# First block's borders by token tiles and column halves, roots with a prepared bias, the MLP's last turn by tiles

## The chip, the cores and the metric

One core of a Trainium2 chip runs the whole program. The metric is the device time of one execution in microseconds (us). TensorE (PE in the rows) does matmuls and transposes, VectorE (DVE) and ScalarE (ACT) the elementwise work, GpSimd (POOL) a little of it, and SyncE (SP) issues all the DMAs, which land in SBUF.

## The reference

Three blocks follow one another on x, 256 tokens of 1024 channels in float32; this case touches only the first, a transformer block of two layers with three kinds of attention. Of each layer, cut to what matters here:

```python
for l in range(DEPTH):                       # DEPTH = 2
    h = _rms_norm(x, norm_mix_pre[l])
    proj = jnp.einsum('bsd,de->bse', h, w_in[l])
    ...                                      # three attentions on parts of proj, gated and mixed
    mixed = jnp.einsum('bsd,de->bse', jnp.sum(gates * br, axis=2), w_out[l])
    x = x + _rms_norm(mixed, norm_mix_post[l])
    h = _rms_norm(x, norm_mlp_pre[l])
    u = jnp.square(jax.nn.relu(jnp.einsum('bsd,df->bsf', h, w_up[l])))
    x = x + _rms_norm(jnp.einsum('bsf,fd->bsd', u, w_down[l]), norm_mlp_post[l])
```

`_rms_norm(x, w)` is `x * rsqrt(mean(x*x) + 1e-6) * w` over the 1024 channels of a token. The second ("even") block begins with a projection of the x that the first leaves.

## The kernel before

Tokens stand in two tiles of 128 partitions (t = 0, 1). Every float32 product is made from three fp32r matmuls (`product`, L379): high times high, low times high and high times low. Weights come in pieces of about 1 MB, each into one of four slots. `load_piece` (L313) issues a piece's DMA on SyncE once the piece that was four before it in the slot is "used"; `high_of_next` (L333) has ScalarE copy it, rounded, into the high part (L344, two halves of 1024 columns), and `low_of_next` (L346) has VectorE subtract that for the low part (L357). Both functions are called at fixed places of each engine's program, two pieces ahead of their use; each engine runs its instructions strictly in program order and waits on counting semaphores. PSUM has 8 banks, which `claim` gives out in turn.

"Border" means here the stretch from the last product of one stage to the first product of the next. There are four of this kind: in each layer from `w_out` ("wo") to the MLP (two), from the first layer's MLP to the second layer's projections, and from the second layer's MLP to the even block. At the first three the same steps follow one another for all 256 tokens at once: ScalarE squares the four banks (two tiles by two column halves, `weigh_scalar`, L1318) with their sums kept, VectorE multiplies them by the norm's weight (`weigh_vector`, L982), a root is made from the sums (`rstd_vector` and `rstd_scalar`: L486, L493, L488), VectorE adds the normed result to x (L994, one instruction of 1024 columns for each tile), ScalarE squares tile 0 of the new x (L1305) and VectorE tile 1 (L965), again a root, VectorE scales both tiles (L970), TensorE transposes them in groups of four 128x128 squares (`turn_tensor`, L459), ScalarE copies the high parts out of PSUM (L468) and VectorE makes the low parts (L478). At the fourth border x is transposed without a norm.

The rows of norm weights are broadcast over the partitions by DMAs of 512 KB. `f.pre` and `f.post` serve both norm pairs, so their MLP rows are issued only when the mix norms are through ("weighed"), and the next layer's pre row when the layer is done ("layer_done").

The MLP runs eight turns. In each TensorE makes two `up` pairs (48 matmuls of 256 columns each) and then multiplies two `down` pieces, j = 0 and 1, with the hidden values, each piece for both tiles and both column halves into four banks held through all turns (`mlp_tensor`, L903). ScalarE and VectorE make the hidden values in between (L1474, L1261, L1479, L1263).

Of the kernel before, what the change touches and what calls it, by code (L numbers as in the profile page):

```python
# [14 lines left out]
P = 128  # L15
S = 256
TT = S // P
D = 1024
# [186 lines left out]
class Kernel:  # L205
# [120 lines left out]

    def load_beyond(self, name):
# [197 lines left out]

FILL_ORDER = [0, 1, 2, 3, 4, 5, 6, (0, 0), (0, 1), 7, 8, 9, (1, 0), (1, 1), 10, 11]
# [15 lines left out]
class FirstPlaces:  # L542
    def __init__(self, k, x):
# [13 lines left out]
        self.stats = take(64)  # L557
# [7 lines left out]
        self.qnT, self.knT = take(4, S), take(4, S)  # L565
        self.heads_out = split(self.pre, TT, WB)
# [29 lines left out]
def first_pieces(k):  # L596
# [8 lines left out]
    for l in range(DEPTH):  # L605
        wi, wo, wu, wd = w_in[:, l], w_out[:, l], w_up[:, l], w_down[:, l]
        for n in range(6):
# [5 lines left out]
            if n == 2:  # L613
# [22 lines left out]
def first_sync(k, f):  # L636
# [13 lines left out]
    for l in range(DEPTH):  # L650
        if l:
            SP.wait_ge(("layer_done", l - 1))
            nc.sync.dma_start(f.pre, row("norm_mix_pre", l)).then_inc(*k.pre_loaded("pre_loaded", l))
# [30 lines left out]
def first_tensor(k, f):  # L684
    nc, T, table = k.nc, k.T, k.table
    for l in range(DEPTH):
        projections_tensor(k, f, l)
        attention_tensor(k, f, l)
        for half in range(2):
            k.token_major(("wo", l, half), k.halves_of(("wo", l, half)), f.hT, WB, lambda t, kk: [("mixed", l, kk // 2 * 2)])  # L690
        k.turn_tensor(("normed", "mlp", l), split(f.flat_junk, TT, D), KT, [[("normed_by", "mlp", l, t)] for t in range(TT)])
        mlp_tensor(k, f, l)

# [18 lines left out]
def projections_tensor(k, f, l):  # L712
    nc, T = k.nc, k.T
    T.wait_ge(("tables_loaded",))
    k.turn_tensor(("normed", "mix", l), split(f.flat_junk, TT, D), KT, [[("normed_by", "mix", l, t)] for t in range(TT)])
    h_ready = k.turned("normed", "mix", l)
    for n in range(6):
        if n in (2, 5):
# [6 lines left out]
        if n == 2:  # L725
# [177 lines left out]
def mlp_tensor(k, f, l):  # L903
    nc, T = k.nc, k.T
    acc = [k.claim("mlp", l, t, half, bank=2 * t + half) for t in range(TT) for half in range(2)]
    for i in range(TURNS):
        for j in range(2):
            k.pair(("up", l, i, j), ("up", l, i, j), f.hT, k.turned("normed", "mlp", l), bank=4 + j)
        for j in range(2):
            p, w = k.weights(("down", l, i, j), 2, D)  # L910
            T.wait_ge(("hidden", l, i, j))
            first, last = i + j == 0, (i, j) == (TURNS - 1, 1)
            for t in range(TT):
                for half in range(2):
                    for kk in range(2):
                        ins = k.product(acc[2 * t + half], [part[:, kk, t * P:(t + 1) * P] for part in f.hidden[j]],
                                        [part[:, kk, half * WB:(half + 1) * WB] for part in w], first and kk == 0, last and kk == 1)
                    if last:
                        ins.then_inc(*T("mlp", l, t, half))
# [25 lines left out]
def first_vector(k, f):  # L945
    nc, V = k.nc, k.V
    nc.vector.memset(f.rel, 1.0).then_inc(*V("rel_ones"))
    for l in range(DEPTH):
        projections_vector(k, f, l)
        attention_vector(k, f, l)  # L950
        for half in range(2):
            k.low_of_next()
            k.low_of_next()
            weigh_vector(k, f, ("mix", l), half, [("wo", l, half, t) for t in range(TT)], ("post_loaded", l))
        add_normed_vector(k, f, ("mix", l))
        normed_vector(k, f, ("mlp", l), ("mlp_rows_loaded", l))
# [3 lines left out]
def normed_vector(k, f, tag, weight_loaded, *ready, pieces=0):  # L960
# [8 lines left out]
    for t in range(TT):  # L969
        nc.vector.scalar_tensor_tensor(normed[:, t, :], x[:, t, :], f.stats[:, 2 + t:3 + t], f.pre, ALU.mult, ALU.mult  # L970
                                       ).then_inc(*V("normed_by", *tag, t))
# [5 lines left out]
def weigh_vector(k, f, tag, half, uses, post_loaded):  # L977
    nc, V = k.nc, k.V
    for t in range(TT):
        at = t * D + half * WB  # L980
        V.wait_ge(("squared", *tag, half, t), post_loaded)
        nc.vector.tensor_tensor(f.flat_junk[:, at:at + WB], k.bank(*uses[t]), f.post[:, half * WB:(half + 1) * WB], ALU.mult  # L982
                                ).then_inc(*V("weighed", *tag, half, t))
        V.same("free", *uses[t])


def add_normed_vector(k, f, tag):
    nc, V, stats, x = k.nc, k.V, f.stats, f.x
    sums = split(stats[:, 0:4], 2, 2)
    nc.vector.tensor_tensor(stats[:, 4:6], sums[:, :, 0], sums[:, :, 1], ALU.add).then_inc(*V())  # L990
    k.rstd_vector(("add", *tag), stats[:, 6:8], stats[:, 4:6], D, EPS_RMS, V)
    V.wait_ge(V)
    for t in range(TT):
        nc.vector.scalar_tensor_tensor(x[:, t, :], f.flat_junk[:, t * D:(t + 1) * D], stats[:, 6 + t:7 + t], x[:, t, :],  # L994
                                       ALU.mult, ALU.add).then_inc(*V("added_to_x", *tag, t))


def projections_vector(k, f, l):
    nc, V, stats = k.nc, k.V, f.stats
    if l == 0:  # L1000
        normed_vector(k, f, ("mix", l), ("pre_loaded", l), ("x_loaded",), pieces=1)
        for _ in range(AHEAD - 1):
            k.low_of_next()
    else:
        normed_vector(k, f, ("mix", l), ("pre_loaded", l))
    for n in range(6):
# [14 lines left out]
        if n == 2:  # L1021
# [232 lines left out]
def mlp_vector(k, f, l):  # L1254
# [11 lines left out]
    for half in range(2):  # L1266
        weigh_vector(k, f, ("mlp", l), half, [("mlp", l, t, half) for t in range(TT)], ("mlp_rows_loaded", l))
    add_normed_vector(k, f, ("mlp", l))
    V.same("layer_done", l)
# [5 lines left out]
def first_scalar(k, f):  # L1275
    nc, A = k.nc, k.A
    for l in range(DEPTH):
        projections_scalar(k, f, l)
        attention_scalar(k, f, l)
        for half in range(2):  # L1280
            k.high_of_next()
            k.high_of_next()
            weigh_scalar(k, f, ("mix", l), half, [("wo", l, half, t) for t in range(TT)])
        k.rstd_scalar(("add", "mix", l), f.stats[:, 6:8])
# [2417 lines left out]
```

## Time and profile before

| | |
|---|---|
| three runs | 1819.9, 1815.75, 1820.47 us; median 1819.9 |
| profiled execution | 1820.19 us, its span 1818.9 us |
| PE busy | 1634.9 us, 90% of the span |
| DVE busy | 1139.2 us, 63% |
| ACT busy | 767.5 us, 42% |
| DMA | 219.94 MB, mean 121 GB/s |
| mean granted TensorE clock | 0.921 |

The span is from the first to the last instruction of the profiled execution; its own time adds 1.3 us around it. Busy shares are means over three blocks with different limits, so what a border costs is read from the timelines of that stretch. Of the chain that ended last, PE holds 72%, DVE 17%, ACT 7% and DMA 3%. In a row of a timeline the brackets give the idle time of the engine before it and what ended it.

### The profile page before, as it was taken

The numbers are of one execution on the slowest core, as the hardware profiler recorded it, in microseconds if no ns is written. First come the engines' busy times: TensorE is split into PE (matmuls) and PEld (weight loads), VectorE is DVE, ScalarE is ACT, GpSimd is POOL, SyncE is SP. The second block draws the span as 40 slices with busy tenths as digits, with TensorE's granted clock in tenths as the row PEclk, the third lists the DMA queues.
The fourth block names the chain that finished last, engine by engine and source line by source line (L and its number), as shares of the span: only waits on it lengthen the run. The fifth ranks groups of instructions, "written<-read, shape, count | busy, mean of one in ns | idle before, by whom it ended". The sixth has DMA issues, their size and how long they took to land.

```text
span 1818.9 us, 24216 instructions
## 1 busy us (share of the span) xinstructions
PE 1634.9 (90%) x10180; PEld 1435.5 (79%) x10180; DVE 1139.2 (63%) x1898; ACT 767.5 (42%) x1260; POOL 53.1 (3%) x50
## 2 busy tenths in 40 slices
PE   7988997999989899979999998987799888999887
PEld 6978886999889888869998987766789767785455
DVE  5577556555546665465556668454977757777765
ACT  4545434444434454344444463422312234645334
POOL 0000011000000000100000001000000000000000
PEclk9999999999989899889999999966877799899998
DMA  8543334555545433245556532000002065331041
GB/s 268 164 140 124 109 105 162 178 189 186 186 136 170 132 122 114 95 139 185 185 186 192 183 110 77 1 1 1 1 1 94 0 209 156 114 129 45 23 156 70
DMA packets 151181, 219.94 MB, mean 121 GB/s; under 512 B 6230, under 2 KB 110686, under 8 KB 150432
## 3 DMA queue, kind: packets, MB, share of 16 engines
q1 hardware_dynamic: 151072, 218.39, 37.6%
q8 instruction: 80, 1.31, 0.3%
q14 instruction: 29, 0.24, 0.0%
HBM read 217.31 MB, written 1.06 MB: 120 GB/s over the span
## 4 chain that ended last, share of the span: by engine, by line
PE 72%; DVE 17%; ACT 7%; DMA 3%; issue 1%; SPq 0%; DVEq 0%
PE bank L381 17%; PE bank L383 16%; PE bank L382 16%; DVE weights_low L357 4%; PE bank L1901 4%; PE bank L846 2%; PE bank L1992 2%; PE bank L3227 2%; ACT weights_high L344 2%; PE bank L2187 2%; DVE place L2381 1%; PE bank L459 1%; PE bank L1958 1%; DMA place<-ple_w_dram 1%; PE bank L3188 1%
## 5 line engine op out<-in xcount | busy, mean ns | idle before, releaser
L357 DVE TENSOR_TENSOR weights_low<-place,weights_high 128x1024 fp32r<-128x1024 f32 (+2 forms) x387 | 450.1, 1206 | 189.4 <-ACT weights_high L344 188.9
L344 ACT ACTIVATE weights_high<-place 128x1024 fp32r<-128x1024 f32 (+2 forms) x387 | 378.7, 1031 | 140.7 <-DMA place<-w_down_dram 42.9
L381 PE MATMUL bank<-hT_high,weights_high 128*128 128x256 f32 x1152 | 336.7, 292 | 6.6 <-DVE hT_low L478 5.0
L383 PE MATMUL bank<-hT_high,weights_low 128*128 128x256 f32 x1152 | 329.2, 286 | 0.0
L382 PE MATMUL bank<-hT_low,weights_high 128*128 128x256 f32 x1152 | 328.7, 285 | 0.0
L381 PEld LDWEIGHTS bank<-hT_high,weights_high 128*128 128x128 f32 x1152 | 222.1, 193 | 12.7 <-DVE hT_low L478 5.8
L382 PEld LDWEIGHTS bank<-hT_low,weights_high 128*128 128x128 f32 x1152 | 221.9, 193 | 0.6
L383 PEld LDWEIGHTS bank<-hT_high,weights_low 128*128 128x128 f32 x1152 | 221.3, 192 | 0.0
L1901 PE MATMUL bank<-place,place 128*128 128x128 f32 x624 | 90.8, 312 | 26.2 <-DVE place L2348 10.4
L1901 PEld LDWEIGHTS bank<-place,place 128*128 128x128 f32 x624 | 87.0, 224 | 33.4 <-issue 22.6
L381 PE MATMUL bank<-weights_high,branchT_high 128*128 128x512 f32 x256 | 101.0, 395 | 0.0
L383 PE MATMUL bank<-weights_high,branchT_low 128*128 128x512 f32 x256 | 101.0, 394 | 0.0
L382 PE MATMUL bank<-weights_low,branchT_high 128*128 128x512 f32 x256 | 101.0, 394 | 0.0
L1424 ACT ACTIVATE place<-place,place 128x256 f32<-128x256 f32 x40 | 20.4, 510 | 144.8 <-DVE place L1155 144.8
L459 PE MATMUL bank<-place,place 128*128 128x128 f32 x144 | 28.1, 367 | 54.5 <-DVE place L970 39.8
L459 PEld LDWEIGHTS bank<-place,place 128*128 128x128 f32 x144 | 24.7, 196 | 58.9 <-DVE place L970 30.9
L1261 DVE TENSOR_TENSOR place<-place 128x512 f32<-128x512 f32 x32 | 22.2, 692 | 74.7 <-ACT place L1474 74.7
L381 PE MATMUL bank<-hT_even_high,weights_high 128*128 128x256 f32 x208 | 61.1, 294 | 3.8 <-DVE weights_low L357 2.5
L381 PE MATMUL bank<-weights_high,hT_high 128*128 128x512 f32 (+1 forms) x160 | 62.1, 388 | 0.8 <-DVE place L1243 0.8
L383 PE MATMUL bank<-weights_high,hT_low 128*128 128x512 f32 (+1 forms) x160 | 61.8, 386 | 0.0
L381 PE MATMUL bank<-branchT_high,weights_high 128*128 128x256 f32 x192 | 57.7, 301 | 4.5 <-ACT place L1401 2.3
L382 PE MATMUL bank<-weights_low,hT_high 128*128 128x512 f32 (+1 forms) x160 | 61.7, 386 | 0.0
(416 smaller groups left out, 3377.1 us busy)
## 6 DMA issues: line engine op xcount, KB each, us to landing
place<-w_in_dram SPq DMA_DIRECT2D x48, 1024.0 KB, 5.3
place<-w_up_dram SPq DMA_DIRECT2D x32, 1024.0 KB, 5.5
place<-w_down_dram SPq DMA_DIRECT2D x32, 1024.0 KB, 5.0
place<-even_w_in_dram SPq DMA_DIRECT2D x17, 1024.0 KB, 5.3
place<-w_out_dram SPq DMA_DIRECT2D x16, 1024.0 KB, 5.1
place<-odd_w_in_dram SPq DMA_DIRECT2D x16, 1024.0 KB, 5.3
place<-w_branch_dram SPq DMA_DIRECT2D x12, 1024.0 KB, 5.0
place<-ple_gate_dram SPq DMA_DIRECT2D x8, 1024.0 KB, 5.9
```

The lines of the kernel that those rows point to most:

```text
L344: nc.scalar.activation(high[:, lo:hi], self.raw[p % SLOTS][:, lo:hi], ACT.Copy).then_inc(*A("high", p, j))
L357: nc.vector.tensor_tensor(low[:, lo:hi], self.raw[p % SLOTS][:, lo:hi], high[:, lo:hi].bitcast(FP32), ALU.subtract).then_inc(*V())
L381: nc.tensor.matmul(out, left[0], right[0], start=first, stop=False)
L382: nc.tensor.matmul(out, left[0], right[1], start=False, stop=False)
L383: return nc.tensor.matmul(out, left[1], right[0], start=False, stop=last)
L459: ins = nc.tensor.transpose(out, tile, self.table("ident"))
L846: ins = nc.tensor.matmul(b[:, at_:at_ + keys], qT[:, q0:q0 + P], kT[:, 0:keys], start=j == 0, stop=j == len(pairs) - 1)
L1261: nc.vector.tensor_tensor(f.u[j], f.u[j], f.u[j], ALU.mult).then_inc(*V("squared_u", l, i, j))
L1901: ins = nc.tensor.matmul(b[:, h * P:(h + 1) * P], left(h), right(h), start=True, stop=True)
L1992: ins = nc.tensor.matmul(b[out, i * width:(i + 1) * width], mats[rows, u, out], right[rows, i, :], start=True, stop=True)
L2187: ins = nc.tensor.matmul(b[:, h * 64:(h + 1) * 64], M[:, h, which, :], right[:, h * 64:(h + 1) * 64], start=not step and j == 0, stop=j == ...
L3227: ins = nc.tensor.matmul(b, left[:, tile, t, :], o.mag[n][hf][:, 0 if real else 1, t, :], start=t == 0, stop=t == TT - 1)
```

## The change

The three borders inside the first block and the one behind it are worked tile by tile and in column halves of 512.

- The second column half of `w_out` is multiplied by `by_tiles_tensor`: tile 0 over both pieces, then tile 1 (before: the first piece for both tiles, then the second). The MLP's last turn likewise: tile 0 with both `down` pieces, then tile 1.
- Weigh, add, square and scale are issued for each tile, in halves. Of each root the mean with epsilon of one column half is prepared on VectorE (`first_mean`), and ScalarE's Sqrt takes it as bias and the other half's sum as input with a scale.
- All squares of the new x are on ScalarE. A Sqrt of one column is put on ScalarE ahead of `w_out`'s first cuts.
- The MLP's norm rows get places of their own (`mlp_pre`, `mlp_post`, over `qnT` and `knT`), and all norm rows are issued earlier in SyncE's queue.
- The cut of the second `up` piece is moved from ahead of the border to behind it.
- The second layer's projections begin with n = 2 (values, token-major) by tiles, and tile 1's transposes are put between its two pieces.

The diff, cut to its core; `weigh_scalar` and the scalar engine's loops are split like the vector engine's.

```diff
+PROJECTIONS = ((0, 1, 2, 3, 4, 5), (2, 0, 1, 3, 4, 5))
...
+        self.mlp_pre, self.mlp_post = (a.rearrange("p a b -> p (a b)") for a in (self.qnT, self.knT))
...
-        k.load_beyond(("wo", l, 1, 1))
-        SP.wait_ge(("weighed", "mix", l, 1, 1), ("headsT", l, 2, 3))
-        nc.sync.dma_start(f.pre, row("norm_mlp_pre", l)).then_inc(*rows())
-        nc.sync.dma_start(f.post, row("norm_mlp_post", l)).then_inc(*rows("mlp_rows_loaded", l))
-        k.load_beyond(("down", l, TURNS - 1, 1))
+        k.load_up_to(("wo", l, 1, 1))
+        SP.wait_ge(("headsT", l, 2, 3))
+        nc.sync.dma_start(f.mlp_pre, row("norm_mlp_pre", l)).then_inc(*rows("mlp_rows_loaded", l))
+        k.load_beyond(("down", l, 0, 1))
+        nc.sync.dma_start(f.mlp_post, row("norm_mlp_post", l)).then_inc(*k.pre_loaded("mlp_post_loaded", l))
+        if l + 1 < DEPTH:
+            nc.sync.dma_start(f.pre, row("norm_mix_pre", l + 1)).then_inc(*k.pre_loaded("pre_loaded", l + 1))
+        SP.wait_ge(("weighed", "mix", l, 1, 1))
+        if l + 1 == DEPTH:
+            k.load_beyond(("down", l, TURNS - 1, 1))
...
+def by_tiles_tensor(k, f, name, ready, between=None):
+
+    T = k.T
+    for t in range(TT):
+        b = k.claim(*name, t)
+        for j, (part, m) in enumerate(k.halves_of(name)):
+            if between and (t, j) == (0, 1):
+                between()
+            p, w = k.weights(part, m, WB)
+            for kk in range(j * m, (j + 1) * m):
+                T.wait_ge(*ready(t, kk))
+                ins = k.product(b, [x[:, kk, t * P:(t + 1) * P] for x in f.hT], [x[:, kk - j * m, :] for x in w], kk == 0, kk == KT - 1)
...
-        for j in range(2):
+        end = i == TURNS - 1
+        for t, j in [(t, j) for t in range(TT) for j in range(2)] if end else [(None, j) for j in range(2)]:
...
+        k.low_of_next()
+        weigh(1, 0)
+        add_normed_vector(k, f, ("mix", l), 0)
+        normed_vector(k, f, ("mlp", l), f.mlp_pre, 0, ("mlp_rows_loaded", l))
+        weigh(1, 1)
+        add_normed_vector(k, f, ("mix", l), 1)
+        k.turn_vector(("normed", "mlp", l), f.hT, KT, 0, [0])
+        normed_vector(k, f, ("mlp", l), f.mlp_pre, 1, ("mlp_rows_loaded", l))
+        k.turn_vector(("normed", "mlp", l), f.hT, KT, 0, [4])
+        k.turn_vector(("normed", "mlp", l), f.hT, KT, 1)
+        k.low_of_next()
         mlp_vector(k, f, l)
...
+def normed_vector(k, f, tag, weight, t, weight_loaded):
+
+    nc, V, stats = k.nc, k.V, f.stats
+    V.wait_ge(("square", *tag, t, 0))
+    nc.vector.tensor_scalar(stats[:, 52 + t:53 + t], stats[:, 48 + 2 * t:49 + 2 * t], 1.0 / D, EPS_RMS, ALU.mult, ALU.add
+                            ).then_inc(*V("first_mean", "norm", *tag, t))
+    V.wait_ge(("deviation", "norm", *tag, t))
+    nc.vector.reciprocal(stats[:, 54 + t:55 + t], stats[:, 54 + t:55 + t]).then_inc(*V())
+    V.wait_ge(V, weight_loaded)
+    for half in range(2):
+        at, cut = t * D + half * WB, slice(half * WB, (half + 1) * WB)
+        nc.vector.scalar_tensor_tensor(f.flat_junk[:, at:at + WB], f.x[:, t, cut], stats[:, 54 + t:55 + t], weight[:, cut],
+                                       ALU.mult, ALU.mult).then_inc(*V("normed_by", *tag, t, half))
...
+        nc.scalar.activation(f.stats[:, 64:65], k.table("ones")[:, 0:1], ACT.Sqrt).then_inc(*A())
...
+    nc.scalar.activation(stats[:, 6 + t:7 + t], stats[:, 2 * t + 1:2 * t + 2], ACT.Sqrt, scale=1.0 / D, bias=stats[:, 4 + t:5 + t]
+                         ).then_inc(*A("deviation", "add", *tag, t))
```

On VectorE, from the last cuts of the first layer's MLP (weights2 and weights3, the second layer's first two pieces) to the first scaling. place23 is the scratch that holds weighed and normed values, place24 the statistics, place14 x, and bank0 to bank3 are the four accumulators. Before:

```order
L357 TENSOR_TENSOR weights2_low_54<-place11_59,weights2_high_53 128x1024 x2
L357 TENSOR_TENSOR weights3_low_56<-place12_60,weights3_high_55 128x1024 x2
L982 TENSOR_TENSOR place23_73<-bank0,place20_70 128x512
L982 TENSOR_TENSOR place23_73<-bank2,place20_70 128x512
L982 TENSOR_TENSOR place23_73<-bank1,place20_70 128x512
L982 TENSOR_TENSOR place23_73<-bank3,place20_70 128x512
L990 TENSOR_TENSOR place24_74<-place24_74 128x2
L486 TENSOR_SCALAR place24_74<-place24_74 128x2
L488 RECIPROCAL place24_74<-place24_74 128x2
L994 SCALAR_TENSOR_TENSOR place14_62<-place23_73,place24_74,place14_62 128x1024 x2
L965 SCALAR_TENSOR_TENSOR place23_73,place24_74<-place14_62 128x1024
L486 TENSOR_SCALAR place24_74<-place24_74 128x2
L488 RECIPROCAL place24_74<-place24_74 128x2
L970 SCALAR_TENSOR_TENSOR place23_73<-place14_62,place24_74,place19_69 128x1024 x2
```

With the change, where place35 is `mlp_post`, line numbers are about 70 higher and the rows of tile 1 follow those of tile 0:

```order
L361 TENSOR_TENSOR weights2_low_54<-place11_59,weights2_high_53 128x1024 x2
L361 TENSOR_TENSOR weights3_low_56<-place12_60,weights3_high_55 128x1024 x2
L1048 TENSOR_TENSOR place23_73<-bank0,place35_85 128x512
L1052 TENSOR_SCALAR place24_74<-place24_74 128x1
L1048 TENSOR_TENSOR place23_73<-bank1,place35_85 128x512
L1059 RECIPROCAL place24_74<-place24_74 128x1
L1063 SCALAR_TENSOR_TENSOR place14_62<-place23_73,place24_74,place14_62 128x512 x2
L1033 TENSOR_SCALAR place24_74<-place24_74 128x1
L1036 RECIPROCAL place24_74<-place24_74 128x1
L1040 SCALAR_TENSOR_TENSOR place23_73<-place14_62,place24_74,place19_69 128x512 x2
L1048 TENSOR_TENSOR place23_73<-bank2,place35_85 128x512
L1052 TENSOR_SCALAR place24_74<-place24_74 128x1
```

Tile 0's weigh, add, root and scaling now stand ahead of tile 1's weigh, all of them still behind the two cuts.

On TensorE, at the same border, with 61 the identity, weights2 and weights3 the first two pieces. Before:

```order
L383 MATMUL bank3<-weights1_high_51,branchT_low_87 128x512
L459 MATMUL bank0<-place13_61,place23_73 128x128 x4
L459 MATMUL bank1<-place13_61,place23_73 128x128 x4
L459 MATMUL bank2<-place13_61,place23_73 128x128 x4
L459 MATMUL bank3<-place13_61,place23_73 128x128 x4
L381 MATMUL bank4<-hT_high_71,weights2_high_53 128x256
L382 MATMUL bank4<-hT_low_72,weights2_high_53 128x256
L383 MATMUL bank4<-hT_high_71,weights2_low_54 128x256
```

With the change (of the twelve products with weights2 the last three stand here):

```order
L387 MATMUL bank3<-weights1_high_51,branchT_low_87 128x512
L463 MATMUL bank0<-place13_61,place23_73 128x128 x4
L463 MATMUL bank1<-place13_61,place23_73 128x128 x4
...
L385 MATMUL bank2<-weights2_high_53,hT_high_71 128x512
L386 MATMUL bank2<-weights2_low_54,hT_high_71 128x512
L387 MATMUL bank2<-weights2_high_53,hT_low_72 128x512
L463 MATMUL bank3<-place13_61,place23_73 128x128 x4
L463 MATMUL bank4<-place13_61,place23_73 128x128 x4
L385 MATMUL bank2<-weights3_high_55,hT_high_71 128x512
```

The products of tile 0 now begin after its own two groups of transposes, and tile 1's groups come between the products of the first and of the second piece.

On ScalarE, from the cuts of `w_out`'s last two pieces (weights0, weights1) to the border in the first layer. Before:

```order
L344 ACTIVATE weights0_high_49<-place9_57 128x1024 x2
L344 ACTIVATE weights1_high_51<-place10_58 128x1024 x2
L1318 ACTIVATE place23_73,place24_74<-bank0 128x512
L1318 ACTIVATE place23_73,place24_74<-bank1 128x512
L344 ACTIVATE weights2_high_53<-place11_59 128x1024 x2
L344 ACTIVATE weights3_high_55<-place12_60 128x1024 x2
L1318 ACTIVATE place23_73,place24_74<-bank2 128x512
L1318 ACTIVATE place23_73,place24_74<-bank3 128x512
L493 ACT_TABLE_LOAD
L493 ACTIVATE place24_74<-place24_74 128x2
L1305 ACTIVATE place23_73,place24_74<-place14_62 128x1024
L493 ACTIVATE place24_74<-place24_74 128x2
```

With the change:

```order
L1358 ACT_TABLE_LOAD
L1358 ACTIVATE place24_74<-place13_61 128x1
L348 ACTIVATE weights0_high_49<-place9_57 128x1024 x2
L348 ACTIVATE weights1_high_51<-place10_58 128x1024 x2
L1423 ACTIVATE place23_73,place24_74<-bank0 128x512
L1423 ACTIVATE place23_73,place24_74<-bank1 128x512
L348 ACTIVATE weights2_high_53<-place11_59 128x1024 x2
L1423 ACTIVATE place23_73,place24_74<-bank2 128x512
L1415 ACTIVATE place24_74<-place24_74 128x1
L1405 ACTIVATE place23_73,place24_74<-place14_62 128x512 x2
L1408 ACTIVATE place24_74<-place24_74 128x1
L1423 ACTIVATE place23_73,place24_74<-bank3 128x512
```

The table load and a one-column Sqrt stand ahead of the two cuts, the cut of weights3 has moved behind the border, and tile 0's Sqrts and squares come ahead of tile 1's first square.

## Rows read from the trace of the kernel before

**Rows 1.** The page's first part: busy time, share, instructions of each engine.

```profile
PE 1634.9 (90%) x10180; PEld 1435.5 (79%) x10180; DVE 1139.2 (63%) x1898; ACT 767.5 (42%) x1260; POOL 53.1 (3%) x50
```

**Rows 2.** Timeline of PE, four borders: start us, us, engine, line.

```profile
310.41 3.33 PE L459 MATMUL bank<-place,place 128*128 128x128 f32 x16 [9.31 <-DVE place L970]
314.73 0.36 PE L381 MATMUL bank<-hT_high,weights_high 128*128 128x256 f32 x1 [1.00 <-DVE hT_low L478]
...
506.32 3.65 PE L459 MATMUL bank<-place,place 128*128 128x128 f32 x16 [10.27 <-DVE place L970]
510.62 0.55 PE L381 MATMUL bank<-hT_high,weights_high 128*128 128x256 f32 x1 [0.65 <-ACT hT_high L468]
...
805.89 3.67 PE L459 MATMUL bank<-place,place 128*128 128x128 f32 x16 [10.07 <-DVE place L970]
810.21 0.55 PE L381 MATMUL bank<-hT_high,weights_high 128*128 128x256 f32 x1 [0.65 <-DVE hT_low L478]
...
997.11 3.67 PE L459 MATMUL bank<-place,place 128*128 128x128 f32 x16 [3.53 <-DVE place L994]
1001.37 0.58 PE L381 MATMUL bank<-hT_even_high,weights_high 128*128 128x256 f32 x1 [0.59 <-DVE hT_even_low L478]
```

**Rows 3.** Timeline of DVE, the border at 301.10 us.

```profile
301.86 0.69 DVE L982 TENSOR_TENSOR place<-bank,place 128x512 f32<-128x512 f32 x1 [2.10 <-ACT place L1318]
...
303.37 0.17 DVE L488 RECIPROCAL place<-place 128x2 f32<-128x2 f32 x1 [0.55 <-ACT place L493]
303.57 2.48 DVE L994 SCALAR_TENSOR_TENSOR place<-place,place,place 128x1024 f32<-128x1024 f32 x2
...
307.84 0.17 DVE L488 RECIPROCAL place<-place 128x2 f32<-128x2 f32 x1 [0.27 <-ACT place L493]
309.06 2.48 DVE L970 SCALAR_TENSOR_TENSOR place<-place,place,place 128x1024 f32<-128x1024 f32 x2 [1.06 <-DMA place<-norm_mlp_post_dram]
...
313.89 1.29 DVE L478 TENSOR_TENSOR hT_low<-bank,hT_high 128x512 fp32r<-128x512 f32 x2 [0.16 <-ACT hT_high L468]
```

**Rows 4.** Timeline of ACT, the same border.

```profile
298.34 0.60 ACT L1318 ACTIVATE place<-bank 128x512 f32<-128x512 f32 x1 [0.89 <-PE bank L383]
...
301.14 0.60 ACT L1318 ACTIVATE place<-bank 128x512 f32<-128x512 f32 x1 [2.11 <-PE bank L383]
...
301.84 1.28 ACT L493 ACT_TABLE_LOAD   x1
...
311.56 0.60 ACT L468 ACTIVATE hT_high<-bank 128x512 fp32r<-128x512 f32 x1 [3.75 <-PE bank L459]
```

**Rows 5.** Timelines of ACT and DVE, end of the first layer's MLP.

```profile
484.89 0.60 ACT L1474 ACTIVATE place<-bank 128x512 f32<-128x512 f32 x1 [1.87 <-PE bank L383]
...
490.15 2.01 ACT L344 ACTIVATE weights_high<-place 128x1024 fp32r<-128x1024 f32 x2 [1.38 <-DMA place<-w_in_dram]
...
486.91 0.69 DVE L1263 TENSOR_TENSOR branchT_low<-place,branchT_high 128x512 fp32r<-128x512 f32 x1 [0.70 <-ACT branchT_high L1479]
...
493.53 0.68 DVE L982 TENSOR_TENSOR place<-bank,place 128x512 f32<-128x512 f32 x1
```

**Rows 6.** Groups of instructions by line: a DVE operation of 512 columns.

```profile
L1604 DVE SCALAR_TENSOR_TENSOR place<-place,bank 128x512 f32<-128x512 f32 x8 | 5.3, 680 | 1.5 <-PE bank L383 1.5
```

**Rows 7.** Timeline of DVE, border of first and second block.

```profile
995.76 2.48 DVE L994 SCALAR_TENSOR_TENSOR place<-place,place,place 128x1024 f32<-128x1024 f32 x2
```

**Rows 8.** Windows of 2 us: PE, PEld, DVE, ACT, POOL busy, granted clock, DMA.

```profile
312.00:314.00 2.00, 1.73 (x10) 1.49 (x8) 1.49 (x3) 1.49 (x4) 0.00 (x0) 0.69 0.00 0
...
514.00:516.00 2.00, 2.00 (x16) 2.00 (x16) 0.00 (x0) 0.00 (x0) 0.00 (x0) 0.84 0.00 0
...
814.00:816.00 2.00, 2.00 (x15) 2.00 (x15) 0.00 (x0) 0.00 (x0) 0.00 (x0) 0.75 0.00 0
```

**Rows 9.** What PE waited for from 310 to 500 us, the whole answer.

```profile
PE bank L459 <- DVE place L970: 9.3, 1, 9.3
PE bank L381 <- DVE hT_low L478: 1.0, 1, 1.0
```

More of the change, by code:

```diff
@@ L908, in mlp_tensor @@
             k.pair(("up", l, i, j), ("up", l, i, j), f.hT, k.turned("normed", "mlp", l), bank=4 + j)
-        for j in range(2):
+        end = i == TURNS - 1
+        for t, j in [(t, j) for t in range(TT) for j in range(2)] if end else [(None, j) for j in range(2)]:
             p, w = k.weights(("down", l, i, j), 2, D)
             T.wait_ge(("hidden", l, i, j))
-            first, last = i + j == 0, (i, j) == (TURNS - 1, 1)
-            for t in range(TT):
+            first, last = i + j == 0, end and j == 1
+            for tile in range(TT) if t is None else [t]:
                 for half in range(2):
                     for kk in range(2):
-                        ins = k.product(acc[2 * t + half], [part[:, kk, t * P:(t + 1) * P] for part in f.hidden[j]],
+                        ins = k.product(acc[2 * tile + half], [part[:, kk, tile * P:(tile + 1) * P] for part in f.hidden[j]],
                                         [part[:, kk, half * WB:(half + 1) * WB] for part in w], first and kk == 0, last and kk == 1)
                     if last:
-                        ins.then_inc(*T("mlp", l, t, half))
+                        ins.then_inc(*T("mlp", l, tile, half))
+            if t == 0:
+                continue
             if last:
@@ L950, in first_vector, with first_normed_vector @@
         attention_vector(k, f, l)
[L951 to L956, printed above, removed]
+        weigh = lambda half, t: weigh_vector(k, f, ("mix", l), f.post, half, t, ("wo", l, half, t), ("post_loaded", l))
+        k.low_of_next()
+        k.low_of_next()
+        for t in range(TT):
+            weigh(0, t)
+        k.low_of_next()
+        weigh(1, 0)
[7 more added lines that the diff above has]
+        k.turn_vector(("normed", "mlp", l), f.hT, KT, 1)
+        k.low_of_next()
         mlp_vector(k, f, l)
-def normed_vector(k, f, tag, weight_loaded, *ready, pieces=0):
+def first_normed_vector(k, f, tag, weight_loaded, *ready, pieces=0):
     nc, V, x = k.nc, k.V, f.x
@@ new lines, in weigh_vector @@
+def weigh_vector(k, f, tag, post, half, t, use, post_loaded):
+    nc, V, stats = k.nc, k.V, f.stats
+    at = t * D + half * WB
+    V.wait_ge(("squared", *tag, half, t), post_loaded)
+    nc.vector.tensor_tensor(f.flat_junk[:, at:at + WB], k.bank(*use), post[:, half * WB:(half + 1) * WB], ALU.mult
+                            ).then_inc(*V("weighed", *tag, half, t))
+    V.same("free", *use)
+    if half == 0:
+        nc.vector.tensor_scalar(stats[:, 4 + t:5 + t], stats[:, 2 * t:2 * t + 1], 1.0 / D, EPS_RMS, ALU.mult, ALU.add
+                                ).then_inc(*V("first_mean", "add", *tag, t))
@@ L1342, in projections_scalar @@
             k.high_of_next()
-        if n == 2:
+        if at == 2:
             if l == 0:
```

159 lines of the change are left out of this document (100 added, 59 removed).

## The prediction, made before the changed kernel ran

> **What bounds the kernel now.** I read the page's first part first: PE is busy for 1634.9 us of an 1818.9 us span [rows 1]. So the time falls where PE stops waiting, and an edit on DVE or ACT is worth what it takes off such a wait. Next I took PE's timeline at the four borders that the change touches. Its bracket gives the idle time before the transposes, so the last product before it ended at E = 310.41 - 9.31 = 301.10, then 496.05, 795.82 and 993.58 us. The first products start at 314.73, 510.62, 810.21 and 1001.37, so the borders last 13.63, 14.57, 14.39 and 7.79 us, together 50.4 us [rows 2]. Then I read what PE waited for between the first two: twice, for the norm (9.3) and for the low part of hT (1.0), never for a weight piece [rows 9]. So the MLP is bound by PE and the borders by a chain over ACT and DVE.
>
> **Prices of the steps**, all at the border of 301.10. ACT's square starts 0.04 after E, and DVE's weigh 0.72 later [rows 3, 4]. A DVE operation of 512 columns takes 0.69, and a scalar_tensor_tensor of 512 columns 0.68 [rows 3, 6], against 1.24 for one of 1024 (2.48 for two) [rows 3]. A DVE instruction after a reciprocal starts 0.20 later. From Sqrt to reciprocal I charge 0.5 with the wait. Squaring 512 columns on ACT with the sum read is 0.8, as a plain ACTIVATE is 0.60. One column half of `w_out` for one tile over one piece is 2.80 us on PE (squares start at 298.34 and 301.14) [rows 4]. From PE's first transpose to ACT's first copy is 1.15 (310.41 to 311.56), from there to DVE's low part 0.63, and from the third low part to the first product 0.84 (313.89 to 314.73) [rows 2 to 4].
>
> **Borders from w_out to MLP.** With E = 0, tile 0 is now done on PE two units of 2.80 earlier, at -5.6. Its weigh runs from -4.85 to -4.15, the reciprocal ends at -3.95, two adds at -2.6, the last square at -1.7, root and reciprocal at -1.2, two scalings at +0.15. Tile 1 then takes: weigh 0.76 to 1.45, reciprocal 1.65, adds 3.0, squares 4.0, root and reciprocal 4.5, first scaling 5.2, four transposes until ACT copies at 6.35, low part from 7.0, first product at 7.85. Low parts of tile 0 fit into DVE's waits. That saves 13.63 - 7.85 = 5.8 and 14.39 - 7.85 = 6.5 us. The wait for a row of norm weights (1.06 us at the first border [rows 3]) is within this.
>
> **The table load.** ACT loads a table for 1.28 us at the border [rows 4], but beside DVE's last weigh and its mean: DVE then waits 0.55 for the root, and 0.27 at the next root, where nothing is loaded [rows 3]. So moving the load is worth 0.3 us in each of the two borders, which the chain above includes. The Trainium skill (ScalarE: Activation LUTs, What ACT_TABLE_LOAD costs) adds a drain of 1380 ns to the 1283 ns of the load. By that the two borders would give 2 x 2.4 = 4.8 us more than by the rows. The trace agrees with the load's length and shows no drain before the Sqrt. At its new place the load and the one-column Sqrt cost ACT 1.5 us ahead of two cuts, which PE first needs 2.8 us apart; hidden. Without that cover it would cost 1.5 us per layer.
>
> **Border from MLP to projections.** Tile 0's results again come 5.6 us early, but the order shows two cuts of weights ahead of them. The second waits for its DMA: ACT cuts it from 490.15 to 492.16, and DVE weighs its first bank at 493.53, 2.52 before E [rows 5]. That stays, since the slot comes free at the same place. So tile 0 takes from -2.5: weigh 0.7, mean 0.2, weigh 0.7, reciprocal 0.2, adds 1.36 (+0.65), squares +1.65, root +2.15, scalings +3.5. Tile 1 queues behind it: weigh, mean, weigh, reciprocal 1.8 (5.3), adds 6.65; then tile 0's low part, and the first product at 6.65 + 0.84 = 7.5. The transposes of tile 1, half of 3.65 us [rows 2], now stand between products: 1.8. The border costs 9.3 against 14.57: 5.3 us saved. Values first, in place of queries, moves no sum: same pieces, same matmuls.
>
> **Border to the even block.** The same start, adds of tile 0 at +0.65; weigh, mean, weigh, reciprocal of tile 1 until 2.45, its adds until 3.8. Today x is added at 995.76 + 2.48 = 998.24 [rows 7], the first product follows 3.13 later. DVE's two memsets and low parts stay in that order, so 3.8 + 3.13 = 6.9 against 7.79: 0.9 us saved.
>
> **Last turns.** Tile 0's product with the second piece needs the second hidden value 2.80 us after the up pair's end (about 484.85) instead of 5.6. It is ready at 486.91 + 0.69 + 0.15 = 487.75 [rows 5], 0.1 late. Twice: 0.2 us lost.
>
> **Hidden work.** Four row loads of 512 KB (three in turn 1 of the first layer's MLP, one before it) come into SyncE's queue among pieces. Two took from 302.55 to 309.06 [rows 3]. PE waits for no piece in the whole MLP [rows 9], so I price them at nothing; their bound is 6.5 us per MB. The slot of the last `down[0]` comes free 2.8 us later, ahead of a border of 9: nothing. The second up piece, cut behind the border, is wanted a pair later: 48 matmuls, about 5.7 us, against 4.4 for both cuts: nothing. Twice as many halves add 0.12 us for each split of 1024, already in the chain.
>
> **The clock.** The granted clock fell in all four borders and rose again at about 313, 514.6, 815 and 1006 us: 0.69, 0.84 and 0.75 in the windows where it did [rows 8]. It did so before the first product only in the first. In the others some 4.1, 4.8 and 4.7 us of products ran at 1.2 in place of 2.4 GHz and lost half: 2.0, 2.4, 2.35, together 6.8 us. In the new borders PE still stands 3.5 us between tile 0's transposes and tile 1's, and again before the products, so I expect it low in all four. That adds up to 2.2 us at the first; I charge 1.5. If it never fell, 6.8 us would come back.
>
> **Sum.** 5.8 + 6.5 + 5.3 + 0.9 = 18.5; less 0.2 and 1.5 makes 16.8. The profiled execution took 1820.2 us, 0.3 above the median of the runs: 1820.2 - 16.8 = 1803.4, I say 1803.
>
> **Rivals.**
> - *The clock stays up.* Longest idle stretch 3.5 instead of 10 us. For it: in the first border it was up again before the products. Against: it fell in every border. 1820.2 - 18.3 - 6.8 = 1795. The Trainium skill (TensorE: Matmul & The Clock Gate, HAM oscillation) says that idle gaps of the kind make the clock fall; no row here shows gaps this short.
> - *The table's drain is real.* 1803.4 - 4.8 = 1799. Against it is DVE's wait of 0.55.
> - *In-order queues eat the lead.* DVE and ACT wait for one another in each tile's chain, and tile 1's square or weigh starts 2 us late in each border: 8 us back, 1811. For it: at the MLP's end tile 1 already queues behind tile 0.
> - *The time comes back later.* PE reaches a piece or a wait of the attention sooner and stands there: the borders shrink, 1817 to 1820. Against: [rows 9].
> - *Slower.* The rows, issued among pieces in a queue kept in order, make pieces late. 3 MB in both layers at 6.5 us per MB is 19.5 us, and slots held 2.8 us longer in two last turns add 5.6: 1820.2 - 16.8 + 25.1 = 1828.5. It decides once 22 us of that reach PE; PE's missing waits for weights speak against it.
>
> **Chances.** Forecast 0.63 (own range 1799 to 1807), clock 0.13, drain 0.05, queues 0.12, back later 0.04, slower 0.03. A measurement of this kernel tells about 0.3%, 5.5 us, from no change. Faster 0.93, same 0.04, slower 0.03. The range takes in the clock case and most of the queues: 1795 to 1809, leaving out under 2 in 10.
>
> **What would show it.** Right: borders of about 7.9, 9.3, 7.9 and 6.9 us from last to first product; no DVE wait for a norm row; DVE's first weigh at the MLP's end still right behind a cut; no PE wait for weights. Wrong: PE waiting for L361 in turn 1 or 2 of the MLP, or in the second layer's projections; a clock that is low for longer than today, or never; tile 1's square late behind tile 0's.

## The result, and the profile after

The changed kernel took 1799.06 us in the median of four runs (1793.44 to 1800.0), the kernel before 1817.83 (1815.52 to 1820.47): a ratio of 0.989, 95% interval 0.9863 to 0.9917. The profiled execution took 1800.00 us with a span of 1798.7, against 1820.19 and 1818.9. The forecast was 1803, its range 1795 to 1809. The medians are 18.8 us apart, the two profiled executions 20.2. A few executions were far slower than the rest (one of 2288.64 us in the first row experiment, one of 3896.85 us of the kernel before), and no median or ratio here rests on them.

The page's busy times hardly moved. VectorE and ScalarE have more and shorter instructions, TensorE the same number as before [rows 1]:

```profile
PE 1632.9 (91%) x10180; PEld 1430.1 (80%) x10180; DVE 1136.8 (63%) x1916; ACT 773.6 (43%) x1287; POOL 53.2 (3%) x50
```

PE's timeline answers to [rows 2]: the first border behind `w_out`, then the one behind the first layer's MLP, then the one to the even block.

```profile
304.81 1.03 PE L463 MATMUL bank<-place,place 128*128 128x128 f32 x8
310.06 1.97 PE L463 MATMUL bank<-place,place 128*128 128x128 f32 x8 [4.22 <-DVE place L1040]
312.58 0.58 PE L385 MATMUL bank<-hT_high,weights_high 128*128 128x256 f32 x1 [0.56 <-DVE hT_low L482]
...
499.81 1.94 PE L463 MATMUL bank<-place,place 128*128 128x128 f32 x8 [2.13 <-DVE place L1040]
503.86 0.77 PE L385 MATMUL bank<-weights_high,hT_high 128*128 128x512 f32 x1 [2.10 <-DVE place L1033]
...
509.11 1.42 PE L463 MATMUL bank<-place,place 128*128 128x128 f32 x8
...
983.08 0.58 PE L385 MATMUL bank<-hT_even_high,weights_high 128*128 128x256 f32 x1 [2.41 <-DVE hT_even_low L482]
```

Tile 0's eight transposes follow the last product at once, and PE then stands 4.22 us for tile 1's. In the second group, products begin after tile 0's transposes, and tile 1's come at 509.11 between products. A table of the whole execution by stages, each number read from PE's timeline (last product, first product, span; rounded, so the last digit can be off by one), shows where the 20.2 us came from:

| stage | before | changed | difference |
|---|---|---|---|
| start to first border | 301.10 | 304.97 | +3.87 |
| border, w_out to MLP | 13.63 | 7.61 | -6.02 |
| MLP of layer 0 | 181.33 | 185.11 | +3.78 |
| border, MLP to projections | 14.56 | 6.17 | -8.39 |
| projections to w_out, layer 1 | 285.19 | 281.64 | -3.55 |
| border, w_out to MLP | 14.40 | 7.71 | -6.69 |
| MLP of layer 1 | 183.38 | 183.78 | +0.40 |
| border to the even block | 7.78 | 6.09 | -1.69 |
| the rest | 817.53 | 815.62 | -1.91 |

The four borders give 22.8 us. The 1.4 us of tile 1's transposes now lie in the stage behind the second border, so the net is 21.4. The other stages take back 1.2 us in all, in pieces of up to 3.9 of either sign. The clock has a large part in them. Behind the first border it was at half speed until 318.8 us, so for 6.2 us of products; before the change it was up before the first product [rows 8]. Windows of the changed kernel behind the first border (engine columns as in [rows 8]):

```profile
312.00:314.00 2.00, 1.44 (x7) 1.42 (x7) 1.58 (x3) 1.94 (x3) 0.00 (x0) 0.50 0.00 0
314.00:316.00 2.00, 2.00 (x12) 2.00 (x11) 2.00 (x3) 2.00 (x3) 0.00 (x0) 0.50 0.00 0
316.00:318.00 2.00, 2.00 (x11) 2.00 (x11) 2.00 (x2) 0.44 (x1) 0.00 (x0) 0.50 0.00 0
318.00:320.00 2.00, 2.00 (x16) 2.00 (x15) 0.27 (x1) 0.00 (x0) 0.00 (x0) 0.81 0.00 0
```

The 3.87 us ahead of the first border are in work that the change hardly touches. In the windows of one such stretch, the first row of before, the second of the changed kernel, PE is busy for the same time, but at a lower clock, and starts 15 matmuls fewer.

```profile
260.00:280.00 20.00, 16.52 (x129) 15.49 (x128) 9.34 (x18) 8.60 (x16) 5.27 (x5) 1.00 0.31 107
260.00:280.00 20.00, 16.52 (x114) 15.73 (x113) 7.49 (x16) 6.62 (x16) 3.57 (x3) 0.83 0.24 77
```

It is not the change's doing. In a later profile of the same changed kernel (r2 below) this stage lasts 301.80 us, 0.70 more than before, and its mean granted clock is 0.99, as before, against 0.98 in the first profile. The stage from the projections to `w_out` is alike: it is 3.55 us shorter than before, at a mean clock of 0.98 in place of 0.95, and in the later profile 1.0 longer, at 0.95 again. So the two pieces of nearly 4 us go with the clock of that execution and not with the change, and it is luck that they cancel.

### The profile page after: what moved, and what is told of

It is laid out like the page before. It is cut to its first block, busy times and chain, and to the rows that moved or that the text cites. A ratio compares the mean times of both kernels' runs of the same rounds, so it can differ in the third digit from the quotient of the medians.

```text
span 1798.7 us, 24270 instructions
## 1 busy us (share of the span) xinstructions
PE 1632.9 (91%) x10180; PEld 1430.1 (80%) x10180; DVE 1136.8 (63%) x1916; ACT 773.6 (43%) x1287; POOL 53.2 (3%) x50
## 4 chain that ended last, share of the span: by engine, by line
PE 70%; DVE 18%; ACT 8%; DMA 2%; issue 1%; SPq 0%; DVEq 0%
PE bank L385 17%; PE bank L386 16%; PE bank L387 16%; DVE weights_low L361 4%; PE bank L2012 3%; PE bank L884 2%; PE bank L2103 2%; ACT weights_high L348 2%; PE bank L3338 2%; PE bank L2298 2%; DVE place L2492 1%; PE bank L2069 1%; DMA place<-ple_w_dram 1%; DMA place<-w_in_dram 1%; PE bank L2276 1%
## 5 line engine op out<-in xcount | busy, mean ns | idle before, releaser
L2012 PE MATMUL bank<-place,place 128*128 128x128 f32 x624 | 89.0, 308 | 26.6 <-DVE place L2459 10.4
L2012 PEld LDWEIGHTS bank<-place,place 128*128 128x128 f32 x624 | 85.0, 219 | 33.7 <-issue 23.0
L1577 ACT ACTIVATE place<-bank 128x512 f32<-128x512 f32 x32 | 19.2, 599 | 100.1 <-PE bank L387 100.1
L386 PE MATMUL bank<-hT_even_low,weights_high 128*128 128x256 f32 x208 | 60.3, 290 | 0.0
```

The lines of the kernel that those rows point to most:

```text
L386: nc.tensor.matmul(out, left[0], right[1], start=False, stop=False)
L2012: ins = nc.tensor.matmul(b[:, h * P:(h + 1) * P], left(h), right(h), start=True, stop=True)
```

## The experiments

All but the row experiment start from the changed kernel. The first row run and the next three experiments ran on one chip, the repeat of the rows, the closer filling, "queries first" and r1 (the changed kernel unaltered) on a second, the late cut, "both" and r2 (again unaltered) on a third. Ratios are to the kernel before on the same chip. Each run has one profile.

**The norm rows alone.** The kernel before gets `mlp_pre` and `mlp_post` and the change's order of loads on SyncE, and nothing else. In short:

```diff
+        self.mlp_pre, self.mlp_post = (a.rearrange("p a b -> p (a b)") for a in (self.qnT, self.knT))
...
-        SP.wait_ge(("weighed", "mix", l, 1, 1), ("headsT", l, 2, 3))
-        nc.sync.dma_start(f.pre, row("norm_mlp_pre", l)).then_inc(*rows())
+        SP.wait_ge(("headsT", l, 2, 3))
+        nc.sync.dma_start(f.mlp_pre, row("norm_mlp_pre", l)).then_inc(*rows("mlp_rows_loaded", l))
```

> The kernel before, with only the places and the early issue of the norm rows taken from the change. Theory (rows hidden among pieces): the three waits for a row, 1.06, 2.26 and 1.83 us, go, PE waits for no weight piece, 5.1 us less than before. Rival (rows make pieces late): the waits go as well, but PE waits for cuts in turn 1 or 2 of the first layer's MLP, and the time is no shorter or longer.

The ratio is 0.9979 (0.9963 to 0.9994), 1811.9 us in the median. The borders are read from the profile of a second run:

> The kernel before with only the places and the early issue of the norm rows, again, for a profile. Theory: no wait of DVE for a norm row at any border, PE waits for no weight piece in the MLPs, borders of 12.6, 12.3, 12.6 and 7.8 us, 4 to 5 us less than before. Rival (rows make pieces late): waits for cuts in turn 1 or 2 of the first layer's MLP.

The second run gave 0.9982 (0.9965 to 1.0). The borders lasted 12.60, 12.33, 12.60 and 7.79 us: 1.03, 2.23 and 1.80 less than before, 5.1 together, as said. The medians fell by 3.3 us on this chip and 3.7 on the other, a little less than the 5.1, and the second interval reaches 1.0; the borders show the gain more surely than the times do. What PE waited for from 310 to 500 us is again no weight piece, and these are all its rows:

```profile
PE bank L463 <- DVE place L977: 8.3, 1, 8.3
PE bank L385 <- DVE hT_low L482: 0.7, 1, 0.7
```

So the rows, issued among the pieces, are hidden, and they account for 5.1 of the 22.8 us, somewhat under a quarter of the borders' gain.

**Product order undone.** The second half of `w_out` and the last turn go back to piece by piece.

```diff
-        by_tiles_tensor(k, f, ("wo", l, 1), lambda t, kk: [])
+        k.token_major(("wo", l, 1), k.halves_of(("wo", l, 1)), f.hT, WB, lambda t, kk: [])
...
-        for t, j in [(t, j) for t in range(TT) for j in range(2)] if end else [(None, j) for j in range(2)]:
+        for t, j in [(None, j) for j in range(2)]:
```

> The changed kernel with TensorE's product order of before in the second half of w_out and in the MLP's last turn; all else stays. Theory (tile 0's lead matters at the w_out borders, where nothing holds it back, and not at the MLP's end, where two cuts stand before it): the two w_out borders grow from 7.7 to about 9.9 us, those behind the MLP stay within 0.3 us of 6.2 and 6.1; 4.4 us more than the changed kernel in all. Rival (the lead is worth 5.6 us a border, or nothing): borders of 10 to 13 everywhere, or 7.7 as now.

Ratio 0.9935 (0.9914 to 0.9956), 1802.8 us. PE's timeline at the first border:

```profile
306.31 1.37 PE L463 MATMUL bank<-place,place 128*128 128x128 f32 x8 [2.32 <-DVE place L1040]
311.16 1.97 PE L463 MATMUL bank<-place,place 128*128 128x128 f32 x8 [3.48 <-DVE place L1040]
313.69 0.58 PE L385 MATMUL bank<-hT_high,weights_high 128*128 128x256 f32 x1 [0.56 <-DVE hT_low L482]
```

From E = 306.31 - 2.32 = 303.99 that is 9.70 us; the other is 9.79. The borders behind the MLPs are 6.42 and 6.22, against 6.17 and 6.09. The theory holds: 4.2 us at `w_out` and 0.4 at the MLPs' ends. (The borders of the unaltered changed kernel lie between 7.25 and 7.71 us at `w_out` in three profiles, between 6.06 and 6.17 behind the MLPs.)

**Table load at the border.** The one-column Sqrt is left out.

```diff
-        nc.scalar.activation(f.stats[:, 64:65], k.table("ones")[:, 0:1], ACT.Sqrt).then_inc(*A())
```

> The changed kernel without the one-column Sqrt ahead of w_out's cuts, so that the table is loaded at the border. Theory (the load of 1.28 us now lies in tile 0's chain, which ends before the last product, so the lead covers it): the two w_out borders grow by 0.3 us or less. Rival (a drain of some 1.4 us stands with the load): ACT is idle for more than 1 us between load and Sqrt, or before the load, and the borders grow by 1 us or more each.

ACT's timeline before the first border, tile 0's Sqrt:

```profile
301.15 0.19 ACT L1422 ACTIVATION_READ_ACCUMULATOR place<-bank 128x1 f32 x1
301.36 1.28 ACT L1414 ACT_TABLE_LOAD   x1
302.66 0.30 ACT L1414 ACTIVATE place<-place 128x1 f32<-128x1 f32 x1
```

The Sqrt starts 0.02 us after the load ends, so there is no drain between them; the load itself starts 0.02 us after the row ahead of it. The borders grew from 7.61 and 7.71 to 7.87 and 8.00 us, 0.3 each. Such a difference is within the scatter of the borders, but the timeline shows its cause: VectorE's scalings of tile 0 now hold it until 307.25, and only then does tile 1's weigh start, 1.03 us after the last product in place of 0.75 (305.72 - 304.97 in the changed kernel). The lead covers all but 0.3 us of the load. The one execution took 1802.48 us, and no interval goes with it.

**Idle stretches filled.** `busy` issues transposes of the identity into a bank that the next real work overwrites, ahead of its wait. They compute nothing that is used.

```diff
+    def busy(self, b, n):
+        for _ in range(n):
+            self.nc.tensor.transpose(b[:, 0:P], self.table("ident"), self.table("ident"))
...
                 b = self.claim(*use, t, g)
+                self.busy(b, busy.get((t, g), 0))
                 T.wait_ge(*(ready(t, g) if callable(ready) else ready[t]))
...
```

> The changed kernel with idle stretches of PE at the four borders filled by transposes of the identity into the bank that the next real work overwrites: 30 before tile 1's transposes behind w_out, 14 and 14 before tile 0's transposes and before the first product at the projections, 11 and 18 before tile 1's transposes and before the first product of the even block. Nothing that counts is computed in them. Theory (the clock falls because PE stands still, and slow products cost 3.1, 3.0, 1.7 and 2.4 us behind the four borders): the granted clock stays at 1.0 through all four and the time falls by 7 to 10 us against the changed kernel. Rival (the clock does not follow from these gaps, or transposes do not hold it up): it falls as before, the time is the same or up to 2 us longer.

Ratio 0.9888 (0.9872 to 0.9904), 1794.2 us. The clock stayed at 1.0 at three borders and was low for 3.4 us of products behind the first, where PE still stood for 0.94 and 0.75 us. The changed kernel unaltered was not on this chip. The run is 21.3 us below the kernel before, and the changed kernel was 18.8, 16.1 and 19.3 below it on other occasions, so the gain is some 2 to 5 us and not the 7 to 10 expected. Then the stretches were filled closer:

> As the run before with filled idle stretches, but filled closer: 37 transposes of the identity before tile 1's behind w_out and 5 before the MLP's first product, 15 and 22 at the projections, 12 and 21 at the even block. Nothing that counts is computed in them. Theory: the clock is 1.0 behind all four borders, the stretches behind them are shorter by what the clock cost there in the changed kernel's profile (3.1, 3.0, 1.7 and 2.4 us), 6 to 10 us less than the changed kernel on the same chip in the median. Rival (slow stretches only move elsewhere, as the clock depends on more than these gaps): the borders are at full clock, but the median gains under 4 us on the changed kernel.

PE's timeline at the first border, the fillers at L455, and one window behind the first product:

```profile
306.46 4.20 PE L455 MATMUL bank<-place 128*128 128x128 f32 x37
310.84 1.32 PE L472 MATMUL bank<-place,place 128*128 128x128 f32 x8 [0.18 <-DVE place L1052]
312.00 0.71 PE L455 MATMUL bank<-place 128*128 128x128 f32 x5
312.92 0.39 PE L385 MATMUL bank<-hT_high,weights_high 128*128 128x256 f32 x1 [0.21 <-DVE hT_low L491]
```

```profile
312.00:314.00 2.00, 1.79 (x16) 1.55 (x15) 1.62 (x4) 1.94 (x4) 0.00 (x0) 1.00 0.00 0
```

All four borders are at full clock. On the same chip the unchanged form of the changed kernel ran too:

> The changed kernel once more, unaltered, on the chip of the next runs. Expected: the same 18 to 21 us below the kernel before. Theory of the clock's part: the four borders last 7.6, 6.2, 7.7 and 6.1 us to 0.1, and what differs between this profile and the first of the changed kernel lies in stretches where the granted clock differs, not in waits. Rival: the borders themselves scatter by more than 0.5 us.

It had 1798.75 us, ratio 0.9909 (0.989 to 0.9929), 16.1 us below the kernel before in place of 18 to 21. Its borders are 7.62, 6.06, 7.51 and 6.10 us, the third 0.2 from the expected one. (Outside its half-speed stretches this profile gives the granted clock as 0.95, a mean of 0.889 in all; no stage is longer for it, so only its half-speed stretches are read here.) The closer filling had 1794.92 us, 0.9894 (0.9875 to 0.9913). The profiles say what the clock costs behind a border: the MLP stages last 182.27 and 182.14 us filled, against 185.11 and 183.78, and 184.75 and 182.77 in the second profile. Of the first pair that is 2.8 and 1.6 us, where 3.1 and 1.7 were expected. But the medians differ by 3.8 us, not by the 6 to 10 expected, and the intervals overlap. By its own bound the rival was right: the borders are at full clock and the gain is under 4 us. What did not come is the gain in the stage from the projections to `w_out`: 283.43 us filled, against 281.64 and 284.01 unfilled. At its start the clock is now up, but the mean over the stage is 0.96, between the 0.98 and 0.95 of unfilled profiles. So slow stretches stand elsewhere in it, in unfilled kernels too (r2 below), and that the filling moved them there is not shown. In the profiles the stages behind the three inner borders together gained 3.7 us on the second profile of the changed kernel (551.53 to 547.84), the borders 1.0.

**Queries first.** `PROJECTIONS[1]` back to 0 to 5, and both tiles' transposes ahead of the first product.

> The changed kernel with the second layer's projections in their old order, queries first, and so with both tiles' transposes ahead of the first product. Theory (VectorE holds tile 1's chain for 3.8 us behind tile 0's first low part, and values first hides it): the border grows from 6.2 us plus 1.4 us of transposes to about 10, 2.4 us more time than the changed kernel. Rival (order of projections moves nothing but the same work): the border grows only by the 1.4 us of transposes, no difference in the sum.

Ratio 0.9918 (0.989 to 0.9946), 1802.5 us. PE's timeline at the second border:

```profile
500.79 1.23 PE L463 MATMUL bank<-place,place 128*128 128x128 f32 x8 [2.32 <-DVE place L1037]
506.29 1.94 PE L463 MATMUL bank<-place,place 128*128 128x128 f32 x8 [4.28 <-DVE place L1037]
508.88 0.55 PE L385 MATMUL bank<-hT_high,weights_high 128*128 128x256 f32 x1 [0.65 <-ACT hT_high L472]
```

From 500.79 - 2.32 = 498.47 the border lasts 10.41 us, against 6.17 + 1.42 = 7.59: values first, with tile 1's transposes between their two pieces, are worth 2.8 us here, and VectorE's chain for tile 1 (4.28 of idle PE) is what they cover. The medians differ by 3.8 us, with intervals that overlap.

**Late cut, and both.** The last turn of the first layer's MLP cuts one piece of the next layer in place of two, and the other is cut behind tile 0's second low part.

```diff
-        for j in range(2):
+        for j in range(1 if l + 1 < DEPTH and i == TURNS - 1 else 2):
             k.low_of_next()
...
         k.turn_vector(("normed", *tag), f.hT, KT, 0, [4])
+        k.low_of_next()
...
```

ScalarE's cuts are moved in the same way.

> The changed kernel unaltered on the chip of the next two runs, as their base: borders of 7.6, 6.1, 7.6 and 6.1 us, 16 to 20 us below the kernel before.

> The changed kernel with the cut of the second layer's second piece moved from ahead of the border behind the MLP to behind tile 0's second low part. Theory (the cut stands before tile 0's chain on ACT and DVE and eats its lead): tile 0 is scaled at about E instead of 2.6 us behind it, the border falls from 6.1 to about 4.2 us, and PE then waits up to 0.9 us for the late cut; 1 us less in all, too little for the clock's scatter. Rival (the lead is held by something else, the squares' and roots' chain): the border stays at 6.1 and PE waits for the cut, 1 to 2 us more.

> The late cut and the closer filling of PE's idle stretches together, the version of which the theories expect most: clock at 1.0 behind the first, third and fourth border, 5 to 8 us below the changed kernel on the same chip. At the second border the 15 and 22 fillers are more than the shorter waits hold, so that the border is about 1 us longer than with the late cut alone. Rival (the clock's slow stretches move elsewhere): under 3 us below the changed kernel.

The base, r2, gave 1793.7 us and 0.9887 (0.9849 to 0.9925), with borders of 7.37, 6.15, 7.25 and 6.09 us, the late cut 1795.3 and 0.9888 (0.9844 to 0.9932), both together 1789.1 and 0.9864 (0.9829 to 0.9899). PE's timeline with the late cut:

```profile
497.93 1.03 PE L463 MATMUL bank<-place,place 128*128 128x128 f32 x8
501.81 0.48 PE L385 MATMUL bank<-weights_high,hT_high 128*128 128x512 f32 x1 [2.84 <-DVE place L1033]
...
506.72 0.51 PE L385 MATMUL bank<-weights_high,hT_high 128*128 128x512 f32 x1 [1.00 <-DVE weights_low L361]
```

The transposes follow the last product without a wait, the border lasts 3.7 us in place of 6.2, and PE waits 1.00 for the cut: the mechanism is as expected and the sizes near it (4.2 and 0.9), the net of 1.5 us is below what the medians can tell (they differ by 1.6 us the other way, within both intervals). Here the clock did not fall at all at this border, though PE was idle for 2.84 us in it. The late cut and the closer filling together are the fastest form of the study, 4.6 us below the changed kernel on one chip in the medians, though the two intervals overlap. That is short of the 5 to 8 expected and more than the rival's 3, so it decides between neither. In its profile the second border lasts 4.67 us, 0.95 longer than with the late cut alone, as expected, and the clock is 1.0 behind all four.

## Why the prediction was right, and where its terms were off

The mechanism was right: the borders shrank by about what was forecast, for the reasons given, and no wait on weights came in return. Two terms of the sum were mis-sized, VectorE's chain behind the MLP and the clock, and one agreement, that of all other stages together, is luck.

**Borders.** Forecast from last to first product 7.85, 7.5, 7.85 and 6.9 us, measured 7.61, 6.17, 7.71 and 6.09; tile 1's transposes 1.8, measured 1.42. The mechanism held at each: tile 0 is through at E behind `w_out`, and the product order is what makes it so (without it 9.70 and 9.79). The term of the borders that was mis-sized is VectorE's chain behind the MLP. I charged 0.7 us for each weigh and 0.2 for each mean, and 0.5 for root and reciprocal. VectorE's timeline shows what they take:

```profile
494.74 0.68 DVE L1048 TENSOR_TENSOR place<-bank,place 128x512 f32<-128x512 f32 x1
495.34 0.15 DVE L1052 TENSOR_SCALAR place<-place 128x1 f32<-128x1 f32 x1
495.40 0.68 DVE L1048 TENSOR_TENSOR place<-bank,place 128x512 f32<-128x512 f32 x1
496.00 0.15 DVE L1059 RECIPROCAL place<-place 128x1 f32<-128x1 f32 x1
496.19 1.42 DVE L1063 SCALAR_TENSOR_TENSOR place<-place,place,place 128x512 f32<-128x512 f32 x2
...
501.69 1.41 DVE L1063 SCALAR_TENSOR_TENSOR place<-place,place,place 128x512 f32<-128x512 f32 x2
503.03 0.68 DVE L482 TENSOR_TENSOR hT_low<-bank,hT_high 128x512 fp32r<-128x512 f32 x1
```

A row's duration is longer than the step to the next start: 0.60 from weigh to mean, 0.06 from mean to weigh, 1.34 for two adds. Weigh, mean, weigh and reciprocal thus take 1.45 us (494.74 to 496.19) where I charged 1.8, once for each tile. Tile 1's adds end 5.35 us after E (503.03 - 497.68), not 6.65. Of these 1.3 us, 0.9 are shorter steps, and 0.4 come from the chain's start, 2.94 us before E in place of 2.52. At the even block it is 0.8 in all. The borders' surplus over the forecast is 2.9 us: these 1.3 and 0.8, 0.4 for the transposes and 0.4 at `w_out`.

**The cuts ahead of the MLP's borders** stood where I put them: the first weigh starts at 494.74, right behind a cut and 2.9 us before E. Moving one of the two cuts took the border to 3.7 us, so it is the cut that held the lead. There the first weigh starts 6.2 us before the last product's end (491.86 to 498.09).

**Table load.** Worth 0.3 us each, as [rows 3] gave; the rival with a drain is out.

**Row loads** at nothing: this held. PE waited for no weight piece from 300 to 1000 us, and in the whole program for 15.2 us in all, against 15.0 before.

**Values first** "moves no sum" was wrong as it stands. My 7.5 us for the border already needed the products of tile 0 to start alone, which they can only do with values first. Undone, it costs 2.8 us.

**Last turns.** In either layer's last turn two products start 0.48 us apart in place of 0.23, so PE waits 0.25 us for the second hidden value, not 0.1. Twice that is 0.5, where 0.2 was charged.

**The clock.** I expected it low in all four new borders, and it was. Products ran slow for 6.2, 6.0, 3.4 and 4.7 us, so 3.1, 3.0, 1.7 and 2.4 us lost, 10.2 in place of 6.8: 3.4 more, where I charged 1.5. I had named a clock that is low for longer than today as a sign of being wrong, and for this term it was one. In r2 they ran slow for 4.9, 5.4, 5.6 and 6.0 us, 11.0 lost, in r1 for 5.6, 5.9, 1.1 and 3.4 us, 8.0 lost. So the cost is 8 to 11 us in all, and its parts change from run to run. Against the rival of a clock that stays up I wrote that no row shows gaps so short; the fourth border of [rows 2] has one, 3.53 us, and the clock fell there.

**The sum.** Forecast 18.5 from the borders, measured 21.4; less 1.2 that all other stages took back, against 1.7 charged. That is 20.2 in place of 16.8 between the profiles, and 18.8 between the medians. The 1.2 near the 1.7 is luck: it is the rest of +3.87, +3.78 and +0.40 against -3.55 and -1.91, less the 1.42 of the transposes, and the first and the fourth of these did not come again in r2. Of the rivals, the queues' eating of the lead was real only as far as the two cuts, which were in the forecast; tile 1's weigh at `w_out` starts 0.75 us after the last product, as charged, and not 2 us late. Nothing came back later as a wait on weights.

## What to carry to other kernels

When an engine waits for a norm over all rows, hand its last products over tile by tile, and then look at what stands in the queues of the engines that take them up: work put there for later eats the lead (here one cut of 2.4 us, worth 2.5 us of border). Split the estimate of such a border into steps from start to start, not durations, since consecutive instructions of VectorE that wait for nothing overlapped by 0.08 to 0.09 us in these rows. Judge a change of this size by the borders in the timeline as well as by the times: the same kernel's other stages differed by up to 4.6 us between two profiles. Put weights that don't wait for the last tile (token-major products) first behind such a border.

## What the runs showed of the hardware

- The scatter of the times goes with the granted clock. The kernel before had 1802.2 to 1822.1 us in eleven runs on one chip, and the fastest had a mean granted clock of 0.933, the slowest 0.916. Between two profiles of the changed kernel, whose borders agree to 0.5 us, the stage from projections to `w_out` differs by 4.6 us (281.64 and 286.20), at a mean clock of 0.98 and 0.95.
- Transposes of the identity held TensorE at 2.4 GHz across a border: 37 and 5 of them with 0.2 us of idle time between kept it at 1.0, while 30 with two stretches of 0.9 and 0.75 did not in one border of two alike. A single stretch of 2.84 us of idle PE passed without a fall (late cut, second border); in r2 one of 2.81, with 2.11 idle shortly before it at the same border, did not.
